# Key and value pages of a paged decoder step loaded as two-page units of 8 KB rows by indirect gathers from GpSimd

## What is computed

```python
def sample_attention(u, c_sb_k, c_sb_v, c_fx_k, c_fx_v, c_logf, page_table, ...):
    gather = lambda cache: cache[page_table].reshape(B, past, *cache.shape[2:])
    ...
    o_sb = stick_breaking(q_sb, k_sb_all, v_sb_all, q_pos, k_pos)
    o_fx = forgetting(q_fx, k_fx_all, v_fx_all, c[:, :, past:], c, q_pos, k_pos)

def stick_breaking(q, k, v, q_pos, k_pos):
    z = einsum('bqhd,bkhd->bhqk', q, k) * SCALE
    log_stay = where(causal, log_sigmoid(-z), 0.0)
    later = cumsum(log_stay, axis=3, reverse=True) - log_stay
    a = where(causal, exp(log_sigmoid(z) + later), 0.0)
    return einsum('bhqk,bkhd->bqhd', a, v)

def forgetting(q, k, v, cq, ck, q_pos, k_pos):
    z = einsum('bqhd,bkhd->bhqk', q, k) * SCALE + cq[..., :, None] - ck[..., None, :]
    return einsum('bhqk,bkhd->bqhd', softmax(where(causal, z, -inf)), v)
```

## Time and profile before

| | |
|---|---|
| median of 3 runs | 1518.41 us (1518.23 to 1520.0) |
| the profiled execution, its own time | 1516.05 us |
| its span, from first to last instruction | 1514.3 us |
| start, to the first step | 0 to 156 us |
| the 128 steps | 156 to about 950 us |
| sample output and experts, to the end | about 950 to 1514 us |
| granted TensorE clock, mean | 0.939 |
| bytes moved by the DMA engines | 570.39 MB |

### The profile page before, as it was taken

The page is one execution under the profiler, slowest core; times in us unless marked ns, Lnnn a source line. Parts: engine busy times, 40 slices in busy tenths (PEclk is TensorE's granted clock), DMA queues, the critical chain, the costliest instruction groups (busy, mean ns, idle before and its releaser), DMA issues. The chain is left out here.

```text
span 1514.3 us, 26133 instructions
## 1 busy us (share of the span) xinstructions
PE 1315.7 (87%) x8622; PEld 870.3 (57%) x8622; DVE 673.4 (44%) x4778; ACT 233.6 (15%) x453; POOL 75.4 (5%) x119
## 2 busy tenths in 40 slices
PE   7999788889789899856899987789999999999992
PEld 4678455566556566533667743466666565655561
DVE  4437855676676675677846466021000100000004
ACT  2111002112212212213011021101111010111011
POOL 1000000000000000001000001001100010001000
PEclk8899989899999999976999998979999999999997
DMA  9776999999999999999999989999999999999984
GB/s 302 248 260 229 385 397 391 396 383 381 382 377 390 383 379 392 387 405 398 351 403 402 401 320 390 399 414 379 422 428 428 427 424 423 422 419 414 416 341 178
DMA packets 170382, 570.39 MB, mean 377 GB/s; under 512 B 17401, under 2 KB 75562, under 8 KB 156954
## 3 DMA queue, kind: packets, MB, share of 16 engines
q1 hardware_dynamic: 145616, 541.70, 91.4%
q10 hardware_dynamic: 21762, 22.58, 4.3%
q0 software_dynamic: 2896, 4.86, 0.9%
HBM read 558.26 MB, written 15.67 MB: 379 GB/s over the span
## 5 line engine op out<-in xcount | busy, mean ns | idle before, releaser
L128 DVE CUSTOM_DVE_ANT_0 ws<-ws,xgT 128x128 f32<-128x128 f32 x1792 | 387.8, 284 | 204.7 <-DMA ws<-in_cache_fox_k 186.0
L979 PE MATMUL bank<-xn,ws 128*128 128x264 f32 x1152 | 289.9, 407 | 10.5 <-DMA ws<-in_w_in 10.5
L979 PEld LDWEIGHTS bank<-xn,ws 128*128 128x128 f32 x1152 | 223.0, 199 | 110.9 <-issue 54.8
L1912 PE MATMUL bank<-ws,xgT 128*64 128x256 f32 x1024 | 231.4, 386 | 16.7 <-DMA ws<-in_w_expert_up 12.1
L1914 PE MATMUL bank<-ws,xgT 128*64 128x256 f32 x1024 | 231.5, 386 | 0.0
L964 PE MATMUL bank<-ws,PR 128*32 128x512 f32 x1024 | 150.8, 668 | 78.3 <-DMA ws<-in_cache_fox_v 73.8
L1912 PEld LDWEIGHTS bank<-ws,xgT 128*64 128x64 f32 x1024 | 140.3, 139 | 104.6 <-issue 22.2
L128 DVE DVE_READ_ACCUMULATOR2_ANT Z<- 128x1 f32 x1792 | 141.8, 79 | 0.0
L1914 PEld LDWEIGHTS bank<-ws,xgT 128*64 128x64 f32 x1024 | 140.3, 139 | 0.0
L2113 DVE COPY gu<-bank 128x256 f32<-128x256 f32 x32 | 13.6, 425 | 269.4 <-PE bank L1914 269.4
L1084 PE MATMUL bank<-qo,ws 128*128 128x256 f32 x512 | 117.0, 387 | 6.2 <-DVE qo L1521 5.2
(11 more groups left out here) (433 smaller groups left out, 971.4 us busy)
## 6 DMA issues: line engine op xcount, KB each, us to landing
ws<-in_cache_sb_k SPq DMA_DIRECT2D x128, 512.0 KB, 9.1
ws<-in_cache_fox_k SPq DMA_DIRECT2D x128, 512.0 KB, 13.0
ws<-in_cache_sb_v SPq DMA_DIRECT2D x128, 512.0 KB, 9.2
ws<-in_cache_fox_v SPq DMA_DIRECT2D x128, 512.0 KB, 12.8
ws<-in_w_expert_gate SPq DMA_DIRECT2D x32, 2048.0 KB, 16.1
ws<-in_w_expert_up SPq DMA_DIRECT2D x32, 2048.0 KB, 20.0
ws<-in_w_expert_down SPq DMA_DIRECT2D x32, 2048.0 KB, 16.9
ws<-in_w_in SPq DMA_DIRECT2D x24, 2048.0 KB, 21.3
```

Of the source, the lines that this page charges most:

```text
L128: ins = dve.tensor_tensor_reduce(k, k, qb[:, (g * H + h) * HD:(g * H + h + 1) * HD], 1.0, 0.0, ALU.mult, ALU.add, Z[:, n % 2, g, h, t:t + 1])
L979: mm = pe.matmul(out[:, 0:T], w[:, c, m * P:(m + 1) * P], xn[:, c, :], start=(c == 0), stop=(c == KC - 1))
L1912: pe.matmul(bank[2 * k][0:SLOTS, 0:256], lhs, ws[:, wg, c * 256:(c + 1) * 256], start=(c == 0), stop=(c == KC - 1))
```

## The change

The cache is now addressed in rows of two tokens: row `r` of a page is tokens `2r` and `2r+1`, 8 KB. A unit is 128 such rows, that is two pages of one cache: the odd page of a pair in partitions 0 to 63, the even one in partitions 64 to 127. A step's work is one unit of one cache instead of one page of both, so even steps take sb, odd steps fox. Each unit is one indirect gather that POOL issues, with the 128 row numbers taken from a column of `prow`, which POOL computes once at the start from the page table. The units of sample 0's keys are still issued by SP, as two direct transfers of 64 partitions x 8 KB each. The rings keep their size. PE uses two value units (four loads before) at every even step. The routing constants are moved into POOL's loop, behind the loads of step 89.

```diff
-def load_key_page(sp, S, kring, caches, ptr, p, n_phys):
-    u = p % 4
+def load_key_unit(pool, S, kring, key_rows, prow, p):
+    u, n, G, g = p % 4, p // PAGES, p % PAGES // 2, p % 2
     if p >= LEAD:
-        sp.wait_ge(S["kused"], p - 3)
-    page = sp.value_load(ptr[0:1, p:p + 1], min_val=0, max_val=n_phys - 1)
-    for k in range(2):
-        sp.dma_start(kring[:, u, k, :], caches[k][bass.ds(page, 1)].rearrange("a p f -> (a p) f")).then_inc(S[f"k{u}"], 16)
+        pool.wait_ge(S["kused"], p - 3)
+    pool.indirect_dma_start(kring[:, u, :], None, key_rows[g],
+                            bass.IndirectOffsetOnAxis(ap=prow[:, n * GROUPS + G:n * GROUPS + G + 1], axis=0)).then_inc(S[f"k{u}"], 16)
...
+def load_value_unit(pool, S, vring, value_rows, prow, p):
+    u, n, G, g = p % 4, p // PAGES, p % PAGES // 2, p % 2
     if p >= 4:
-        sp.wait_ge(S["vused"], p - 3)
...
+        pool.wait_ge(S["vused"], p - g - 2)
...
+def score_unit(dve, kunit, qb, Zg, g, G):
+    for j in range(2):
+        for h in range(H):
+            k = kunit[:, (j * H + h) * HD:(j * H + h + 1) * HD]
+            ins = dve.tensor_tensor_reduce(k, k, qb[:, (g * H + h) * HD:(g * H + h + 1) * HD], 1.0, 0.0,
+                                           ALU.mult, ALU.add, Zg[:, h, 2 * G + j:2 * G + j + 1])
...
-HALF_POS = [i % 4 for i in range(20)] + [0, 1, 4, 5, 6, 7, 2, 3, 0, 1, 4, 5]
+UNIT_POS = [i % 2 for i in range(10)] + [0, 2, 3, 1, 0, 2]
...
+                def key_unit(i):
...
+                    if before:
                         sp.wait_ge(A["hused"], before[-1] + 1)
+                    for half in range(2):
+                        t = 2 * G + 1 - half
+                        page = sp.value_load(ptr[0:1, t:t + 1], min_val=0, max_val=n_phys - 1)
+                        sp.dma_start(kring[64 * half:64 * half + 64, u, :],
+                                     key_caches[g][bass.ds(page, 1)].rearrange("a r f -> (a r) f")).then_inc(A[f"kh{u}"], 16)
...
-                for half in range(2):
-                    out = bank[2 + half]
-                    pe.matmul(out[:, :], tri_gt[:, :], LFT[:, half * 512:(half + 1) * 512], start=True, stop=False,
-                              skip_group_check=True)
-                    for k in range(4):
...
+                for b in range(2):
+                    lft = LFT[:, b * 512:(b + 1) * 512].rearrange("p (m q) -> p m q", q=2)
+                    for half in range(2):
+                        out = bank[2 + b][64 * half:64 * half + 64, :]
+                        for j in range(2):
+                            pe.matmul(out.rearrange("p (m j) -> p m j", j=2)[:, :, j], tri_in[:, j, :], lft[:, :, 1 - half],
+                                      start=(j == 0), stop=False, skip_group_check=True)
+                        for k in range(4):
+                            mm = pe.matmul(out[:, k * P:(k + 1) * P], totb[:, b * 4 + k, 0:64],
...
@@ SP, in the steps @@
-            for s in range(STEPS):
-                if s == 8:
-                    sp.wait_ge(A["lst"], 32)
-                if s >= 4:
-                    load_value_page(sp, S, vring, value_caches, ptr, s, n_phys)
-                if s + LEAD < STEPS:
-                    load_key_page(sp, S, kring, key_caches, ptr, s + LEAD, n_phys)
-                if s % 4 == 3 and 7 <= s < 8 * TURNS - 1:
-                    i = (s - 7) // 4
...
+            sp.wait_ge(A["lst"], 32)
+            for i in range(2 * (TURNS - 1)):
+                sp.wait_ge(S["evac"], 2 * i + 2)
...
@@ POOL, in the steps @@
+            pool.wait_ge(A["rows"], 1)
+            pool.wait_ge(A["q_done"], 10)
+            for p in range(2):
+                load_value_unit(pool, S, vring, value_rows, prow, p)
+            for p in range(PAGES, LEAD):
...
+                load_key_unit(pool, S, kring, key_rows, prow, p)
+            pool.wait_ge(A["q_done"], 12)
+            for p in range(2, 4):
+                load_value_unit(pool, S, vring, value_rows, prow, p)
+            for s in range(STEPS):
+                if s >= 4 and s % 2 == 0:
+                    load_value_unit(pool, S, vring, value_rows, prow, s)
+                if s + LEAD < STEPS:
+                    load_key_unit(pool, S, kring, key_rows, prow, s + LEAD)
+                if s >= 4 and s % 2 == 0:
+                    load_value_unit(pool, S, vring, value_rows, prow, s + 1)
+                if s == GSUM + 8:
+                    routing_constants()
...
@@ PE, values(s), now called at even s @@
-                pe.wait_ge(S[f"v{u}"], 32 * (s // 4 + 1))
+                for g in range(2):
+                    pe.wait_ge(S[f"v{s % 4 + g}"], 16 * (s // 4 + 1))
+                for j in range(2):
+                    for g in range(2):
+                        for half in range(2):
...
+                mm.then_inc(S["vused"], 2)
...
@@ DVE, sample_logs and sample_exponents @@
-                own.step(dve.tensor_tensor(sp_h[:, :, 1:PAGES + 1], by_head(zr[:, :]), by_head(zs[:, :]), ALU.add))
+                own.step(dve.tensor_tensor(sp_a[:, :, :], by_head(zr[:, :]), by_head(zs[:, :]), ALU.add))
+                own.step(dve.tensor_tensor(sp_h[:, :, 1:GROUPS + 1], sp_a[:, :, 0:PAGES:2], sp_a[:, :, 1:PAGES:2], ALU.add))
...
+                odd_t = by_head(ts[:, :])[:, :, 1:PAGES:2]
+                dve.tensor_tensor(odd_t, odd_t, sp_a[:, :, 0:PAGES:2], ALU.add).then_inc(S["ts"], 1)
```

More of the change, by code:

```diff
@@ L647, in vector @@
                 dve.wait_ge(A["fg"], FG["fb"])
+                dve.wait_ge(A["rows"], 1)
                 for i in range(2):
@@ L653, in vector @@
                 dve.tensor_copy(fpart[:, :], bank[6][:, 0:T]).then_inc(A["fgc"], 1)
-                for i in range(5):
-                    score_half(i)
+                for i in range(2):
+                    score_first(i)
                 dve.wait_ge(A["fg"], FG["f"])
@@ L664, in vector @@
                 own.step(dve.tensor_scalar(fr[:, :], fl[:, :], -1.0, 0.0, ALU.mult, ALU.max))
-                for i in range(5, 9):
-                    score_half(i)
+                for i in range(2, 4):
+                    score_first(i)
                 dve.wait_ge(A["fln"], 1)
@@ L669, in vector @@
                                          in1=fa[:, :], op0=ALU.mult, op1=ALU.subtract).then_inc(A["fgc"], 1)
-                for i in range(9, PAGES):
-                    score_half(i)
+                for i in range(4, GROUPS):
+                    score_first(i)
                 dve.wait_ge(A["fg"], FG["ct"])
@@ L682, in vector @@
                                        sp_h[:, :, :].rearrange("p h j -> p (h j)"), 0.0, ALU.mult, ALU.add).then_inc(S["ssp"], 1)
-                for i in range(PAGES, 2 * PAGES):
-                    score_half(i)
-                    if i == PAGES:
+                for i in range(GROUPS, 2 * GROUPS):
+                    score_first(i)
+                    if i == GROUPS:
                         dve.wait_ge(A["fg"], FG["c2s"])
-                        dve.scalar_tensor_tensor(out=ts[:, :], in0=z_sb, scalar=SCALE, in1=bank[1][:, P:2 * P],
-                                                 op0=ALU.mult, op1=ALU.subtract).then_inc(S["ts"], 1)
+                        own.step(dve.scalar_tensor_tensor(out=ts[:, :], in0=z_sb, scalar=SCALE, in1=bank[1][:, P:2 * P],
+                                                          op0=ALU.mult, op1=ALU.subtract))
+                        tv = ts[:, :].rearrange("p (h j) -> p h j", j=PAGES)[:, :, 1:PAGES:2]
+                        dve.tensor_tensor(tv, tv, sp_a[:, :, 0:PAGES:2], ALU.add).then_inc(S["ts"], 1)
@@ L929, in _ @@
-            own.step(pool.memset(manyf[:, :], 1.0))
-            own.step(pool.iota(io32[:, :].rearrange("p (h d s) -> p h d s", h=2, d=2), [[HALF, 2], [0, 2], [1, HALF]],
-                               base=0, channel_multiplier=0))
-            own.step(pool.tensor_copy(slot2_of[:, :], io32[:, :]))
-            for i in range(3):
-                own.step(pool.tensor_scalar(dtmp[:, i:i + 1], tok[:, 0:1], float(HALF * (i + 1)), None, ALU.is_ge))
-            own.step(pool.tensor_tensor(dtmp[:, 3:4], dtmp[:, 0:1], dtmp[:, 1:2], ALU.subtract))
@@ L936, in _ @@
-            own.step(pool.tensor_tensor(dtmp[:, 3:4], dtmp[:, 3:4], dtmp[:, 2:3], ALU.add))
-            own.step(pool.tensor_scalar(drow[:, :], dtmp[:, 3:4], float(4 * T), None, ALU.add))
-            own.step(pool.tensor_scalar(dtmp[:, 0:1], dtmp[:, 0:1], -float(HALF), None, ALU.mult))
-            own.step(pool.tensor_tensor(tok[:, 2:3], tok[:, 2:3], dtmp[:, 0:1], ALU.add))
-            for k in range(2):
-                own.step(pool.tensor_scalar(destc[:, :, k], tok[:, :], -2.0, float(4 * T - 2 * T * k), ALU.mult, ALU.add))
@@ new lines, in _ @@
+            pool.wait_ge(A["rows"], 1)
[3 more added lines that the diff above has]
+            for p in range(PAGES, LEAD):
+                last = max(i for i in range(2 * GROUPS) if UNIT_POS[i] == p % 4)
+                if last < 2 * GROUPS - 1:
```

(4 more changed lines are left out.)

212 lines of the change are left out of this document (111 added, 101 removed).

## The result

| | before | after |
|---|---|---|
| median of 4 runs each, us | 1518.58 (1518.23 to 1520.0) | 1646.87 (1640.21 to 1650.66) |
| the profiled execution / its span, us | 1516.05 / 1514.3 | 1647.34 / 1645.6 |
| start: to the first sum over the scores | 152.0 | 186.4 |
| steps: from there to the last of the eight | 744.1 | 829.4 |
| end: from there to the end of the span | 618.2 | 629.8 |

A forecast was written before the change was run, and what follows sets the result against it. Transfers were taken to bound most of the steps, with PE near its limit late and full at the start; -15 + 4.4 + 2.6 = -8 us, from 1518.4 to 1510 us, range of 8 in 10 from 1495 to 1540 us.

The forecast's parts named there:

- Rival 2: Steps: `w_in` in 1 KB pieces starves beside 8 KB pieces; +24 - 8, 1534 us; chance 0.04.
- The start's key loads: Start: sample 0's keys in transfers of 64 partitions instead of 128; +2.6 us taken, between 0 and +8.
- The sums of log forget values: Start, on PE: these sums send twice the columns through PE, on the path to step 0; +4.4 us.
- Larger pieces: Cache page transfers: 8 KB pieces instead of 4 KB, and 240 transfers less; -15 us.
- rival 3: Gathers: each row moves in two pieces, so only the start's 7 us are left; 1525 us; chance 0.04.
- The issue on POOL: Steps: two gathers of about 1.17 us each fit into a step of 6.7 us on POOL; 0 us.
- Rival 1: Steps: POOL's gathers and DVE's scores shut each other out; +24 us with the start, 1543 us; chance 0.22.

The follow-up runs named there:

- e5: Changed kernel, but POOL issues the 16 `w_in` loads of the steps in its own order instead of SP: 1573.36 us.
- e4: Changed kernel with e1 and e5 together: POOL gathers sample 0's keys over 128 partitions and issues `w_in` in its order: 1545.17 us.
- e9: e4, with the first eight and four of the last six `w_out` blocks also issued in POOL's order: 1525.41 us, ratio 1.0048 to the kernel before.
- e2: Changed kernel, but each `w_in` load in the steps is issued in two halves, one by SP and one by ACT: 1586.98 us.
- e1: Changed kernel, but sample 0's 16 key units are gathered by POOL into all 128 partitions, not loaded by SP in halves of 64: 1629.02 us.
- e10: Kernel before, but each of sample 0's key pages is loaded as two transfers of 64 partitions: 1533.32 us, ratio 1.0114.
- e13: e11, with the first eight `w_out` blocks also issued in POOL's order: 1533.46 us.
- e11: e3, with the `w_in` blocks also issued in POOL's order: 1542.15 us.
- e14: Kernel before, but the first eight `w_out` blocks are issued by SP in its own order instead of ACT: 1519.26 us, ratio 1.0007.
- e3: Kernel before, but in the steps POOL issues the cache pages as 480 gathers of 4 KB rows, leaving `w_in` alone in SP's queue: 1546.67 us.

## Why the prediction was wrong, point by point

**Rival 2, small pieces starve beside large ones: right as a mechanism, wrong in its price and its chance, and the main cause.** I had 24 us and a chance of 0.04. Of the steps' time it held 73.9 us by `w_in` (e5) and 19.5 more by `w_out` (e4 to e9). Together that is 93.4 us, more than the steps lost, because the larger piece's gain lay under it. The step of the prediction that failed is the sentence that "PE waits for it instead of for values and the engines never rest". The rings hold only four units each, and POOL fills them within the time in which `w_in` is held up. After that nothing is left to load until PE moves on, DVE behind it and POOL behind DVE: a share of 0.20 from 410 to 420 us. A late block isn't exchanged for an early value. It stops the engines that free the buffers, and the DMA engines idle behind them. I had worked out 46 us for a block that is due every 26.7 us, and so had the number that contradicted the small price. I then took 1.5 us for each of 16 loads without a row for it; PE waited 135.8 us over nine.

The Trainium skill, DMA: Bandwidth & Descriptors, Queues, rings and completion order, says that a DMA engine goes round the queues that have work, taking a packet of several descriptors, up to 64, from each. The rounds are seen here, but 503 packets against 504, and 836 against 837, show turns of one packet of the trace each, and on SyncE's queue such a packet was one row of 1 KB. The Trainium skill, DMA: Bandwidth & Descriptors, Rules for kernel authors, says that spreading transfers over several issuing engines doesn't help bandwidth, since they share the DMA engines. In e2 it took 59.6 us off the steps all the same, because it bought `w_in` more turns.

**The start's key loads: +2.6 taken, +8 as the upper end.** They cost 24.3 us here (e1) and 13.9 in the kernel before (e10). That each transfer takes twice as long was the upper bound's assumption, and it holds: 214 and 226 GB/s. What failed is the set-off against 33 us of idle DMA time in the stage. That time isn't free to take. The first ten units go through two slots, each loaded again once the unit in it has been scored, and the first fox units can't be scored before their query is there. DVE's wait for it, from 40 to 162 us of the kernel after, and SyncE's key loads around it:

```profile
DVE ws L123 <- ACT xgT L476: 22.4, 1, 22.4
...
104.41 4.36 SPq L325 DMA_DIRECT2D ws<-in_cache_fox_k  x4
...
137.49 23.11 SPq L325 DMA_DIRECT2D ws<-in_cache_fox_k  x12
```

Between these two rows no key load was issued: SyncE waited 27.4 us for DVE to score the unit in the next slot. And from 130 to 150 us the DMA share is 0.31. In the kernel before, the idle time lies at the same place (0.17 from 110 to 130 us, with a wait of 14.0 us for the query). The last six units then follow, from 150 us on at half rate and a full share. What more slots would have saved wasn't tried. The rule of the Trainium skill, SBUF — State Buffer, Door 1: The DMA port swizzle (a transfer into partitions 0 to 63 reaches half of the ports), agrees with these rates; I had cited it for +8 and put it aside.

**The sums of log forget values: +4.4 taken.** They took 7.2 us instead of 4.35, so +2.9. Why twice the columns cost less than twice the time, no run shows. From PE's timeline after, first and the instruction behind the last:

```profile
44.80 1.97 PE L560 MATMUL bank<-blk,ts 128*64 128x256 f32 x4
...
52.02 1.32 PE L572 MATMUL bank<-xn,PR 128*32 128x264 f32 x20
```

**Larger pieces: -15.** Right in size, once nothing small ran beside: 15.0 us between e13 and e9, 8.4 between e11 and e4. Piece and unit changed together in these pairs, so the gain is that of both. Rows of 8 KB did move whole: of the 37456 packets of POOL's queue, 30,720 are of 8 KB, 128 for each of the 240 units. So rival 3 fell.

**The issue on POOL: 0.** Not quite. With the same piece and everything in one order, POOL's gathers make steps of 750.4 us (e13) where SyncE's transfers make 743.4 (e14), and the end is 5 to 15 us longer than before in every kernel with gathers. I had looked only at whether POOL has the time. A gather takes 0.94 us of POOL and the next follows 0.30 us behind, so a pair takes 2.5 us from the moment when its buffers are free, and where values are all that is left this may come on top. That this is what the end lost is argued from these times; no run shows it apart.

**Rival 1, POOL and DVE exclude each other: not seen.** The gathers' own row, and a score of 281 ns:

```profile
L105 POOL DMA_INDIRECT ws<-in_cache_sb_k,prow x56: 932/938/3431, 180.1 to 976.3; - x56
L105 POOL DMA_INDIRECT ws<-in_cache_fox_k,prow x56: 932/941/1017, 181.4 to 981.2; - x56
```

One of these 112 was held up, at 3431 ns; of the 128 gathers of values none took over 1157 ns. The rule that I put beside it, in the Trainium skill, SBUF — State Buffer, SBUF: two separate sides, does not bear on these gathers, or they read too little of SBUF to meet it; the runs don't tell which. I had given 0.22 to the rival that a rule and one row of another instruction spoke for, and 0.04 to the one for which the earlier trace rows had a measured rate and a due time.

**What stays open.** Of the end's 11.6 us, the values' later arrival explains some 10 (60.2 against 49.9 us); why even e9 has 10.0 is explained in part, by 6.2 us more of PE's waits for values and 2.3 for the expert pick's additions on POOL, which stood behind POOL's last waits. Of the start, 9.7 us are left in e9; 2.9 are the log-forget sums and 5.0 are PE's waits for the heads' `w_in` chunks (12.1 against 7.1 us from 30 to 165 us). The rest wasn't tried.

## What to carry to other kernels

Before giving one stream a queue of its own, compare its piece with that of the stream beside it: bytes are shared by piece, not by need, so weights in 1 KB pieces beside 8 KB gathers get an eighth; either keep both in one order or give the small one more queues. Price a late transfer by who frees the buffers: if it stops the engine that does, the other stream stops too, and here the loss was four times what I had worked out from the delay (93 against 24 us). And check the partitions of each transfer before its piece size: over 64 of them it ran at 214 to 226 GB/s, over 128 at 386 to 413, and with few slots idle DMA time does not hide that.

## What the runs showed of the hardware that was not expected

- Two queues with work alternate packet by packet, whatever the sizes: 503 and 504 in 10 us (8 KB and 1 KB), 836 and 837 (4 KB and 1 KB), and at no point between were the counts over five apart.
- The same rows of 1 KB are one packet each on SyncE's queue and four to a packet on POOL's (e5). On average from 200 to 640 us, a packet of 4 KB made of them took 188 ns (e5), and four of 1 KB on SyncE's queue took 193 ns (the kernel after).
- An engine's issue of a transfer can block it for as long as its queue is behind: 22.67 us for a store of 128 KB behind two `w_out` blocks. A like hold-up of 14.35 us in the kernel before cost nothing that e14 could find.
- A gather of 128 rows of 8 KB is issued by GpSimd in 938 ns while DVE scores, one of 4 KB rows in 943 ns (e3), and moves each row in one piece.
- Pieces of 1 KB are dearer by the byte, but not by much. From 405 to 415 us of the kernel after, by queue, `w_in`'s 1.79 MB took 55.1% of the engines, which is 325 GB/s at a full share, and the gathers' 0.70 MB took 17.0%, 412 GB/s:

```profile
q1 hardware_dynamic: 1764, 1.79, 55.1%
q0 software_dynamic: 102, 0.70, 17.0%
```
